# Six weight pairs loaded in the merge, products in TensorE's waits, and half of the branch weights issued earlier

## The chip, the core and the metric

The kernel runs on one core of a Trainium2 chip. The metric is device time in microseconds (us) of one execution; the time before is the median of three runs. One further execution was profiled, and all rows here are from it. The engines are TensorE (PE; PEld is its weight load), VectorE (DVE), ScalarE (ACT), GpSimd (POOL) and SyncE (SP, which issues most DMAs; "SPq" in rows). Each issues on its own, in program order, and they wait for each other by semaphores.

## What is computed

One decoder layer for 256 prompt tokens and 8 sample tokens (264 in all), model width 1024, in f32:

```
p = rms_norm(x) @ w_in
x = x + (sig(g_a) * (rwkv(p) @ w_br_a) + sig(g_b) * (nsa(p) @ w_br_b)) @ w_out
h = rms_norm(x)
logits = h @ w_router + b_router            # 32 experts, top 4, softmax
x = x + sum over the 4 experts:  top_w * (clamped_swiglu(h @ w_up[e] + b_up[e]) @ w_down[e] + b_down[e])
y = rms_norm(x)
```

`rwkv` is an RWKV-7 recurrence, `nsa` a sparse attention with a compressed, a selected and a window branch over cached keys. One expert has w_up of 1024x2048 (8.4 MB) and w_down of 1024x1024 (4.2 MB); all 32 are read, 403 MB. The sample group's window cache, shifted by a row, is an output too (a copy of 4.2 MB from memory to memory).

## The kernel before

The program is a row of stages; each is a block that begins and ends with a barrier of all engines. The order inside a block is written out by hand, engine by engine.

- `rwkv()` (projection and recurrence), then `attend()` with `compress` (compressed keys and values; `layer1`, the products L1135, and at its end L1188 and L1193), `attend_prompt` (begins with L1347, then gate products L1356 between attention products), `attend_samples` and `merge`.
- In `attend_samples` SyncE loads window rows, waits for `turned` to reach 16 and issues w_br_a and w_br_b (four loads each, L1479) into the half 0:P of every row of `sel`, where turned keys stood. TensorE turns the keys of eight (group, sample quad) units, and after them runs `branch_a(0)` (L1632) with w_br_a.
- In `merge` SyncE issues w_out (eight loads of [128, 8, 128], L1698) into the other half of `sel`, then x again and seven small loads (L1702, L1708, the last is c_dest), then the four quarters of w_up of expert 0 (L185). GpSimd waits for all of those but w_up and then issues the copy of the window cache (L1718). TensorE multiplies by w_br (L1764), by w_out (L1776), adds x (L1778), and makes partial logits (L1784) and sums of squares (L1789).
- In `experts` SyncE first issues the biases and a table `pick`, each twice (L1858 to L1860, semaphore `bias_in`, 96 in all), then w_down of experts 0 and 1 (four loads, L1854, in `sp_routes`), then w_up of expert 1, and then in a loop the weights of all others, each load when the slot is free. TensorE turns h (L2022), ranks the assignments (L2028, L2030), gathers expert 0's rows by a product (L2036), makes the table of slots (L2043), then runs expert 0: bias products (L2417), w_up products (L2430), later w_down (L2451) and the addition back (L2405). VectorE waits for `bias_in` after its one-hot work, copies `pick` twice (L1931, L1932), counts, and multiplies the gathered rows by the norm's gain (L1958); only then can L2430 begin.

Expert weights go through a ring of eight buffers `pairs` (16 KB per partition each, "ring" in rows): 0 to 3 hold the four quarters of one w_up, 4 to 7 two experts' w_down in halves. Pairs 4 to 7 lie over `sel`, so while w_out is there they can't be loaded. A quarter of w_up or a half of w_down is one DMA of 2 MB (2,097,152 bytes).

Of the kernel before, what the change touches and what calls it, by code (L numbers as in the profile page):

```python
# [29 lines left out]
P = 128  # L30
D = 1024
# [73 lines left out]
def build(nc, a, o, scratch):  # L105
    ctx = ExitStack()
    with ctx:
# [75 lines left out]
        def upper_weights(sp, e):  # L183
            for q in range(4):
                sp.dma_start(pairs[q][:], a["w_up"][0][e, 256 * q:256 * q + 256, :].rearrange("(p c) n -> p c n", c=2)).then_inc(ring_in[2 * q], 16)  # L185

# [31 lines left out]
        halves_of = (slice(0, HD), slice(HD, P))  # L218

# [403 lines left out]
        def rwkv_chunks(ar, q, bk, wc, av, br, vt, ktt, r, v):  # L623

            with nc.Block() as block, ExitStack() as st:
# [145 lines left out]
                def _(pe):  # L771
# [125 lines left out]
                    mm.then_inc(so, 1)  # L897

# [26 lines left out]
        def compress(sel, rows, qg, yb, B0, B1, gtok, bin_):  # L925


            with nc.Block() as block, ExitStack() as st:
# [196 lines left out]
                def _(pe):  # L1125
# [40 lines left out]
                    for b in range(NR // 2):  # L1166
                        if b % 2 == 0:
                            pe.wait_ge(C["raw_in"][b // 2], 32)
                        for r in (2 * b, 2 * b + 1):
                            if r >= 3:  # L1170
                                pe.wait_ge((fl_a, fl_d)[(r - 3) % 2], 2 * ((r - 3) // 2) + 1)
                            for kv in range(2):
                                for t in range(2):
                                    c0 = 256 * (r % 4) + P * kv
                                    mm = nc.tensor.transpose(banks[r % 3][:, TP * kv + P * t:TP * kv + P * t + P], raw[b // 2][:, t, c0:c0 + P], ident)
                            mm.then_inc(turned, 1)
                        if 2 * b in at_half:
                            setup(at_half.index(2 * b))
                        if b:
                            layer1(2 * b - 2)  # L1180
                            layer1(2 * b - 1)
                        if 2 * b + 1 in at_half:
                            setup(at_half.index(2 * b + 1))
                    layer1(NR - 2)
                    layer1(NR - 1)
                    pe.wait_ge(gl_ok, 2)
# [7 lines left out]
                    mm.then_inc(vc, 1)  # L1194

# [234 lines left out]
        def attend_samples(sel, qg, yb, B1, sc_, sel_in, br_in):  # L1430


            with nc.Block() as block, ExitStack() as st:
# [38 lines left out]
                def _(sp):  # L1472
# [3 lines left out]
                    sp.wait_ge(turned, 16)  # L1476
                    for i, n in enumerate("ab"):
                        for c in range(4):
                            sp.dma_start(sel[:, 4 * i + c, :, :, 0:P], a[f"w_br_{n}"][0][P * c:P * c + P, :].rearrange("p (a b n) -> p a b n", a=2, b=4)).then_inc(br_in[i], 16)  # L1479
# [198 lines left out]
        def merge(sel, br_in):  # L1678

            with nc.Block() as block, ExitStack() as st:  # L1680
# [11 lines left out]
                root_w = at("table_of_root", [P, 1], TEMPS)  # L1692
                wo_in, x_again = sem("mg_w_out_in"), sem("x_in_again")

                @block.sync
                def _(sp):
                    for c in range(KD):
                        sp.dma_start(sel[:, c, :, :, P:256], a["w_out"][0][P * c:P * c + P, :].rearrange("p (a b n) -> p a b n", a=2, b=4)).then_inc(wo_in, 16)  # L1698
# [11 lines left out]
                    upper_weights(sp, 0)  # L1710
# [43 lines left out]
                def _(pe):  # L1754
# [15 lines left out]
                    for m in range(KD):  # L1770
                        if m >= 2:
                            pe.wait_ge(oe, m - 1)
                        for c in range(KD):
                            if m == 0 and c == KD - 1:
                                pe.wait_ge(mix_ok, KD)
                            mmul(banks[m % 2][:, 0:T], sel[:, c, m // 4, m % 4, P:256], mix[:, c, :], start=(c == 0), stop=False)  # L1776
# [13 lines left out]
                    mm.then_inc(partd, 1)  # L1790

# [24 lines left out]
        def route(st):  # L1816
# [33 lines left out]
            def sp_routes(sp):  # L1850
                def down(e):
                    for j in range(2):
                        slot = 8 + 4 * e + 2 * j
                        sp.dma_start(pairs[slot // 2][:], a["w_down"][0][e, 512 * j:512 * j + 512, :].rearrange("(p b c) n -> p b (c n)", b=2, c=2)).then_inc(ring_in[slot], 16)  # L1854

# [5 lines left out]
                down(0)  # L1861
                down(1)
# [147 lines left out]
            def pe_routes(pe):  # L2010
                mmul = nc.tensor.matmul
                for lo, signal in ((1, msd), (0, lgd)):
# [3 lines left out]
                    mm.then_inc(signal, 1)  # L2016
                for i in range(6):
# [13 lines left out]
                mm.then_inc(rkd, 1)  # L2031
                for t, (_, n) in enumerate(TILES):
# [543 lines left out]
```

## Time and profile before

| what | us |
|---|---|
| median of three runs | 1440.2 |
| lowest and highest | 1438.92, 1441.64 |
| the profiled execution's own time | 1438.51 |
| its span in the trace | 1436.6 |

Mean granted TensorE clock 0.974 of full speed (full is 2.4 GHz, the lower level 0.5 of it is 1.2 GHz). TensorE is busy 93% of the span; of the chain that ended last, waits for DMAs are 33% and TensorE 32%. Stages in the profile: recurrence to 200 us, compressed branch to 273.7, prompt attention to 376, samples to 413.9, merge to 474.8, routing and experts from there. A row of a timeline gives the start, the length, the engine, the line and the operation, with the number of merged instructions; an f32 product counts as two. In brackets is the idle time before it and what ended it.

### The profile page before, as it was taken

How to read it: one execution, taken by the hardware profiler on the slowest of the kernel's cores; microseconds unless marked ns; L12 is line 12 of the kernel's file. 1: busy time of each engine (PE TensorE's matmuls, PEld its weight loads, DVE VectorE, ACT ScalarE, POOL GpSimd, SP SyncE). 2: the span in 40 equal slices, each digit the busy share in tenths (PEclk: the TensorE clock that was granted, in tenths of full speed). 3: DMA queues.
4: the chain of work that ended last, by engine and by line, in shares of the span. 5: the costliest groups of instructions: out<-in, count | busy, mean ns of one | idle time of the engine just before them, and what ended most of it. 6: DMA issues, size and time to landing. Idle time of an engine off the chain costs nothing.

```text
span 1436.6 us, 20588 instructions
## 1 busy us (share of the span) xinstructions
PE 1336.5 (93%) x8365; PEld 663.5 (46%) x8366; DVE 495.3 (34%) x1055; ACT 189.9 (13%) x407; POOL 101.9 (7%) x150
## 2 busy tenths in 40 slices
PE   6998879899999989999999999999999999999995
PEld 6887867687778523332333233333333333233231
DVE  3455556424551413232323223224222322233224
ACT  3221113323410300000000000000000000000001
POOL 1002032330000000000000000000000000000000
PEclk9999989899999999999999999999999999999998
DMA  6333248184488899999999999999999999999993
GB/s 213 118 93 91 64 108 269 41 276 146 150 215 341 337 431 429 431 430 431 431 431 431 431 431 432 430 430 431 431 429 433 430 432 431 431 432 430 431 431 133
DMA packets 94195, 479.94 MB, mean 334 GB/s; under 512 B 12740, under 2 KB 61110, under 8 KB 69176
## 3 DMA queue, kind: packets, MB, share of 16 engines
q1 hardware_dynamic: 85832, 452.00, 77.7%
q0 software_dynamic: 7600, 25.45, 4.9%
q10 hardware_dynamic: 704, 1.63, 0.3%
q8 instruction: 46, 0.75, 0.2%
q14 instruction: 13, 0.11, 0.0%
HBM read 478.60 MB, written 8.56 MB: 339 GB/s over the span
## 4 chain that ended last, share of the span: by engine, by line
DMA 33%; PE 32%; DVE 1%; issue 1%; ACT 0%; SPq 0%; DVEq 0%; ACTq 0%
DMA ring<-in_w_up 33%; PE bank L2430 18%; PE bank L2451 7%; PE bank L2405 2%; PE bank L2444 1%; PE bank L2417 1%; DVE x L2268 1%; PE bank L2387 1%; PE bank L2036 0%; PE bank L2022 0%; PE bank L2393 0%; DVE ring L2356 0%; PE bank L2043 0%; DVE x L2365 0%; PE bank L2014 0%
## 5 line engine op out<-in xcount | busy, mean ns | idle before, releaser
L2430 PE MATMUL bank<-ring,ex_work 128*64 128x512 f32 x2048 | 464.9, 603 | 24.4 <-DMA ring<-in_w_up 24.4
L2430 PEld LDWEIGHTS bank<-ring,ex_work 128*64 128x64 f32 x2048 | 140.9, 138 | 333.9 <-issue 274.3
L2451 PE MATMUL bank<-ring,ex_work 128*64 128x512 f32 x1024 | 233.6, 610 | 0.0
L2279 DVE TENSOR_SCALAR ex_work<-bank 128x512 f32<-128x512 f32 x32 | 22.1, 691 | 401.6 <-PE bank L2430 401.6
L2268 DVE TENSOR_TENSOR x<-bank,x 128x512 f32<-128x512 f32 (+1 forms) x192 | 117.2, 670 | 101.5 <-PE bank L2405 101.5
L2451 PEld LDWEIGHTS bank<-ring,ex_work 128*64 128x64 f32 x1024 | 72.2, 140 | 159.1 <-issue 159.1
L2405 PE MATMUL bank<-ex_work,ex_back 64*128 64x512 f32 x384 | 91.1, 606 | 1.5 <-ACT ex_work L2199 1.5
L558 PE MATMUL bank<-hT,w_group 128*128 128x264 f32 (+1 forms) x400 | 90.1, 387 | 0.0
L558 PEld LDWEIGHTS bank<-hT,w_group 128*128 128x128 f32 (+1 forms) x400 | 74.3, 186 | 14.7 <-issue 0.7
L2161 POOL DMA_INDIRECT ex_work<-scratch_h,ex_si x31 | 31.7, 1022 | 603.1 <-PE bank L2387 602.3
L2193 ACT ACTIVATE ex_work<-ex_work 128x512 f32<-128x512 f32 x32 | 20.1, 629 | 382.0 <-DVE ex_work L2279 382.0
L1356 PE MATMUL bank<-hT,w_cmp 128*128 128x264 f32 x256 | 67.8, 410 | 0.0
L2275 DVE COPY ex_pick_down<-ex_pick 64x64 f32 (+1 forms) x31 | 5.8, 187 | 162.4 <-PE bank L2451 162.4
L2405 PEld LDWEIGHTS bank<-ex_work,ex_back 64*128 64x128 f32 x384 | 34.4, 186 | 57.8 <-issue 49.8
L2199 ACT ACTIVATE ex_work<-bank 128x512 f32<-128x512 f32 x32 | 19.1, 597 | 262.8 <-PE bank L2451 262.8
L1356 PEld LDWEIGHTS bank<-hT,w_cmp 128*128 128x128 f32 x256 | 48.8, 201 | 7.4
L2189 ACT ACTIVATE ex_work<-bank 128x512 f32<-128x512 f32 x32 | 19.1, 597 | 227.4 <-PE bank L2393 227.4
L2444 PE MATMUL bank<-ex_bias,ex_pick_down 32*64 32x512 f32 x128 | 34.4, 612 | 15.9 <-DVE x L2268 14.5
L2417 PE MATMUL bank<-ex_bias,ex_pick_up 32*64 32x512 f32 x256 | 34.8, 612 | 0.6 <-DVE ex_pick_up L2271 0.6
L1776 PE MATMUL bank<-mixed,sel_rows 128*128 128x264 f32 x128 | 30.4, 391 | 0.0
L2387 PEld LDWEIGHTS bank<-masks,ex_work 128*128 128x128 f32 x124 | 17.3, 208 | 26.3 <-issue 23.5
L1958 DVE TENSOR_TENSOR ex_work<-bank,gain_columns 128x256 f32<-128x256 f32 x64 | 23.9, 413 | 9.5 <-PE bank L2387 8.0
(485 smaller groups left out, 1180.8 us busy)
## 6 DMA issues: line engine op xcount, KB each, us to landing
ring<-in_w_up SPq DMA_DIRECT2D x128, 2048.0 KB, 24.1
ring<-in_w_down SPq DMA_DIRECT2D x64, 2048.0 KB, 26.8
w_group<-in_w_in SPq DMA_DIRECT2D x12, 1024.0 KB, 5.3
w_cmp<-in_w_in SPq DMA_DIRECT2D x8, 1024.0 KB, 8.7
sel_rows<-in_w_out SPq DMA_DIRECT2D x8, 512.0 KB, 7.3
out_win_s<-in_state_win_kv POOLq DMA_DIRECT2D x1, 4088.0 KB, 28.9
x<-in_x_prompt SPq DMA_DIRECT2D x4, 512.0 KB, 4.9
win_rows<-in_state_win_kv SPq DMA_DIRECT2D x4, 512.0 KB, 4.9
```

Source lines behind the costliest of these rows:

```text
L558: mm = mmul(banks[2 + i % 4][0:n, 0:T], w[:, g % 3, kc, c:c + n], hT[:, kc, :], start=(kc == 0), stop=(kc == KD - 1))
L1356: mm = mmul(gate_bank(t)[:, 0:T], w[:, t // 2 % 2, kc, P * (t % 2):P * (t % 2) + P], C["hT"][:, kc, :], start=(kc == 0), stop=(kc == KD - 1))
L1776: mmul(banks[m % 2][:, 0:T], sel[:, c, m // 4, m % 4, P:256], mix[:, c, :], start=(c == 0), stop=False)
L1958: ins = nc.vector.tensor_tensor(B["xT"][:, :, gs], bank.rearrange("p (k s) -> p k s", k=4)[:, :, gs], R["gcol"][:, 2 * g:2 * g + 2].rearra ...
L2161: pool.indirect_dma_start(B["xg"][:], None, halves(scratch["h"]), bass.IndirectOffsetOnAxis(ap=B["si"][:, 0:1], axis=0), bounds_check=last ...
L2268: nc.vector.tensor_tensor(dst, banks[bank][0:n, :], dst, ALU.add).then_inc(S["added"], 1)
L2387: mm = nc.tensor.transpose(banks[6][:, P * k:P * k + P], B["xg"][:, 256 * (k // 2):256 * (k // 2) + 256].rearrange("s (p c) -> s c p", c=2 ...
L2405: mm = mmul(banks[bank], B["back"][hs, P * t:P * t + P], B["y"][hs, :], start=True, stop=True)
L2417: mmul(banks[n // 2][lo:lo + SLOTS, :], B["pick_up"][es, :], B["bias"][es, 512 * n:512 * n + 512], start=True, stop=False)
L2430: mm = mmul(banks[n // 2][lo:lo + SLOTS, :], B["xT"][:, k % 4, SLOTS * (k // 4):SLOTS * (k // 4) + SLOTS], slot_of(k)[:, 512 * n:512 * n + ...
L2444: mmul(banks[4][SLOTS * n:SLOTS * n + SLOTS, :], B["pick_down"][0:NEXP, :], B["bias"][0:NEXP, 2 * FF + 512 * n:2 * FF + 512 * n + 512], st ...
L2451: mm = mmul(banks[4][SLOTS * n:SLOTS * n + SLOTS, :], B["hT"][:, k % 4, SLOTS * (k // 4):SLOTS * (k // 4) + SLOTS], slot_of(8 + 4 * half + ...
```

## The change

- `merge` loads w_out into ring pairs 2 and 3, whole rows of 4 KB, not into `sel`. So `sel` is free once the branch products are done, and SyncE then (`ab`, KD) issues w_down of experts 0 and 1 into pairs 4 to 7. Of w_up of expert 0 only quarters 0 and 1 are issued before that, and quarters 2 and 3 after the output products (`od`, KD). `sp_routes` keeps the biases alone.
- `filled(bank, n)`: n products `ident` by 256 columns of `masks` into a bank that is not in use, at seven places.
- w_br_a is issued when eight units' keys are turned, w_br_b at sixteen as before.

```diff
-        def upper_weights(sp, e):
-            for q in range(4):
+        def upper_weights(sp, e, parts):
+            for q in parts:
...
+        def lower_weights(sp, e):
+            for j in range(2):
+                slot = 8 + 4 * e + 2 * j
+                sp.dma_start(pairs[slot // 2][:], a["w_down"][0][e, 512 * j:512 * j + 512, :].rearrange("(p b c) n -> p b (c n)", b=2, c=2)).then_inc(ring_in[slot], 16)
...
+        def filled(bank, n):
+            for _ in range(n):
+                nc.tensor.matmul(bank[:, 0:2 * P], ident, masks[:, 0:2 * P], start=True, stop=True)
...
                     mm.then_inc(so, 1)
+                    filled(banks[6], 4)
...
+                        if b == 1:
+                            filled(banks[3], 2)
                         if 2 * b in at_half:
...
                     layer1(NR - 1)
+                    filled(banks[2], 4)
                     pe.wait_ge(gl_ok, 2)
...
                     mm.then_inc(vc, 1)
+                    filled(banks[2], 2)
...
-                    sp.wait_ge(turned, 16)
                     for i, n in enumerate("ab"):
+                        sp.wait_ge(turned, 8 + 8 * i)
                         for c in range(4):
...
+                def wo(c):
+                    return pairs[2 + c // 4][:, c % 4 // 2, D * (c % 2):D * (c % 2) + D]
...
-                        sp.dma_start(sel[:, c, :, :, P:256], a["w_out"][0][P * c:P * c + P, :].rearrange("p (a b n) -> p a b n", a=2, b=4)).then_inc(wo_in, 16)
+                        sp.dma_start(wo(c), a["w_out"][0][P * c:P * c + P, :]).then_inc(wo_in, 16)
...
                     sp.wait_ge(outs.sem, 16 * 9)
-                    upper_weights(sp, 0)
+                    upper_weights(sp, 0, (0, 1))
+                    sp.wait_ge(ab, KD)
+                    for e in range(2):
+                        lower_weights(sp, e)
+                    sp.wait_ge(od, KD)
+                    upper_weights(sp, 0, (2, 3))
...
-                            mmul(banks[m % 2][:, 0:T], sel[:, c, m // 4, m % 4, P:256], mix[:, c, :], start=(c == 0), stop=False)
+                            mmul(banks[m % 2][:, 0:T], wo(c)[:, P * m:P * m + P], mix[:, c, :], start=(c == 0), stop=False)
...
                     mm.then_inc(partd, 1)
+                    filled(banks[7], 1)
...
-                down(0)
-                down(1)
...
                     mm.then_inc(signal, 1)
+                filled(banks[6], 2)
                 for i in range(6):
...
                 mm.then_inc(rkd, 1)
+                filled(banks[6], 2)
```

SyncE, from the end of the merge's small loads to the first load of expert 1; ring0 to ring3 are the quarters of w_up, ring4 to ring7 the halves of w_down. Before:

```order
L1708 DMA masks<-in_c_dest 128x24
L185 DMA ring0_49<-in_w_up 128x4096
L185 DMA ring1_50<-in_w_up 128x4096
L185 DMA ring2_51<-in_w_up 128x4096
L185 DMA ring3_52<-in_w_up 128x4096
L1680 UNCONDITIONAL_BRANCH
...
L1860 DMA ex_pick_4810<-in_c_pick 32x33
L1854 DMA ring4_53<-in_w_down 128x4096
...
L1854 DMA ring7_56<-in_w_down 128x4096
L2110 DMA ring0_49<-in_w_up 128x4096
```

And now:

```order
L1725 DMA masks<-in_c_dest 128x24
L185 DMA ring0_49<-in_w_up 128x4096
L185 DMA ring1_50<-in_w_up 128x4096
L190 DMA ring4_53<-in_w_down 128x4096
...
L190 DMA ring7_56<-in_w_down 128x4096
L185 DMA ring2_51<-in_w_up 128x4096
L185 DMA ring3_52<-in_w_up 128x4096
L1694 UNCONDITIONAL_BRANCH
...
L1878 DMA ex_pick_4830<-in_c_pick 32x33
L2128 DMA ring0_49<-in_w_up 128x4096
```

The w_down loads moved ahead of the stage's end, and so ahead of the biases; quarters 2 and 3 of w_up moved behind them.

TensorE at the end of the compressed branch, where the lines L1201 and L1206 are L1188 and L1193 of before, now:

```order
L1145 MATMUL bank<-sel_rows,w_cmp_late 128x265 x8
L227 MATMUL bank<-masks 128x256 x4
L1201 MATMUL bank<-sel_rows,w_cmp 64x264 x2
L1206 MATMUL bank<-w_cmp,sel_rows 128x64 x4
L1206 MATMUL bank<-w_cmp,sel_rows 8x64 x2
L227 MATMUL bank<-masks 128x256 x2
L938 UNCONDITIONAL_BRANCH
```

The two L227 rows are new; the rest stands as before.

## Rows read from the trace of the kernel before

**Rows 1.** The page, chain that ended last by line; then its last long wait.

```profile
DMA ring<-in_w_up 33%; PE bank L2430 18%; PE bank L2451 7%; PE bank L2405 2%; PE bank L2444 1%; PE bank L2417 1%; DVE x L2268 1%; PE bank L2387 1%; PE bank L2036 0%; PE bank L2022 0%; PE bank L2393 0%; DVE ring L2356 0%; PE bank L2043 0%; DVE x L2365 0%; PE bank L2014 0%
...
1318.41 25.93 DMA ring<-in_w_up
```

**Rows 2.** The page, GB/s moved in slices of 36 us.

```profile
GB/s 213 118 93 91 64 108 269 41 276 146 150 215 341 337 431 429 431 430 431 431 431 431 431 431 432 430 430 431 431 429 433 430 432 431 431 432 430 431 431 133
```

**Rows 3.** The issue of expert 1's first w_up quarter, with its time to landing.

```profile
L2110 SPq DMA_DIRECT2D ring<-in_w_up x1: 328/328/328, 496.3 to 496.3; - x1
...
DMA to landing us min/median/max: 14.6/14.6/14.6
```

**Rows 4.** Timeline of VectorE and TensorE before expert 0.

```profile
487.02 0.18 DVE L1931 COPY ex_pick_up<-ex_pick 64x64 f32<-64x64 f32 x1
...
489.92 0.76 DVE L1958 TENSOR_TENSOR ex_work<-bank,gain_columns 128x256 f32<-128x256 f32 x2 [1.47 <-PE bank L2050]
...
492.63 13.95 PE L2430 MATMUL bank<-ring,ex_work 128*64 128x512 f32 x64
```

**Rows 5.** Expert 0's w_up: issues 1 and 2, then all four, with landings.

```profile
L185 SPq DMA_DIRECT2D ring<-in_w_up x2: 432/432/433, 435.6 to 436.1; - x2
...
DMA to landing us min/median/max: 7.8/19.8/31.9
...
L185 SPq DMA_DIRECT2D ring<-in_w_up x4: 432/484/1137, 435.6 to 437.7; - x4
...
DMA to landing us min/median/max: 7.8/34.1/42.6
```

**Rows 6.** The window copy: its issue on GpSimd, and size and landing from the page.

```profile
439.18 0.68 POOL L1718 DMA_DIRECT2D out_win_s<-in_state_win_kv  x1 [24.32 <-DMA masks<-in_c_dest]
...
out_win_s<-in_state_win_kv POOLq DMA_DIRECT2D x1, 4088.0 KB, 28.9
```

**Rows 7.** Stretches; the last three columns are granted clock, DMA share, GB/s.

```profile
382.00:384.00 2.00, 2.00 (x23) 1.50 (x21) 1.58 (x3) 1.72 (x5) 0.00 (x0) 1.00 1.03 424
418.00:420.00 2.00, 2.00 (x10) 1.62 (x9) 1.51 (x4) 0.00 (x0) 0.00 (x0) 1.00 1.11 286
470.00:472.00 2.00, 2.00 (x28) 1.70 (x30) 0.43 (x1) 0.39 (x1) 0.00 (x0) 1.00 0.48 205
```

**Rows 8.** Timeline of SyncE's issues.

```profile
413.89 11.77 SPq L1698 DMA_DIRECT2D sel_rows<-in_w_out  x8
...
474.84 0.33 SPq L1858 DMA_DIRECT2D ex_bias<-in_b_up  x1
```

**Rows 9.** The last of the bias loads, the second pick table, with its landing.

```profile
L1860 SPq DMA_DIRECT2D ex_pick<-in_c_pick x1: 421/421/421, 477.1 to 477.1; - x1
...
DMA to landing us min/median/max: 6.9/6.9/6.9
```

**Rows 10.** Expert 1's first w_up products; the clock there; as many products later.

```profile
511.04 8.78 PE L2430 MATMUL bank<-ring,ex_work 128*64 128x512 f32 x32 [0.20 <-DMA ring<-in_w_up]
...
511.00:514.00 3.00, 2.96 (x8) 1.12 (x10) 0.00 (x0) 0.00 (x0) 0.00 (x0) 0.50 1.01 431
...
549.82 7.02 PE bank L2430 x32
```

**Rows 11.** Timeline of TensorE, four branch products of 264 columns.

```profile
433.61 1.94 PE L1764 MATMUL bank<-yaT,sel_rows 128*128 128x264 f32 x8
```

**Rows 12.** TensorE from the end of the compressed branch; then two stretches.

```profile
269.08 0.67 PE L1188 MATMUL bank<-sel_rows,w_cmp 128*64 128x264 f32 x4 [2.14 <-ACT sel_rows L1040]
269.83 1.43 PE L1193 MATMUL bank<-w_cmp,sel_rows 128*128 128x64 f32 x12
273.76 3.59 PE L1347 MATMUL bank<-KcT,pT 64*128 64x8 f32 x32 [2.51 <-PEq L928]
...
272.00:275.00 3.00, 1.24 (x12) 1.27 (x13) 0.00 (x0) 0.00 (x0) 1.11 (x6) 0.50 0.05 10
...
278.00:282.00 4.00, 4.00 (x11) 3.07 (x10) 1.43 (x6) 0.00 (x0) 0.20 (x2) 0.50 0.00 0
```

**Rows 13.** The wait for w_br_a on TensorE, and ScalarE's second exponential.

```profile
399.59 2.05 PE L1632 MATMUL bank<-yaT,sel_rows 128*128 128x264 f32 x8 [2.17 <-DMA sel_rows<-in_w_br_a]
...
401.86 0.72 ACT L1499 ACTIVATE bias<-bias,s_max 128x513 f32<-128x513 f32 x1 [0.99 <-DVE s_max L1558]
```

More of the change, by code:

```diff
@@ L1850, in sp_routes @@
             def sp_routes(sp):
[L1851 to L1854, printed above, removed]
                 for i in range(2):
```

## The prediction

> **What bounds the kernel now.** I read the views from the end backwards. The chain of work that ended last is a third wait for w_up ("DMA ring<-in_w_up 33%"), and its last such wait lasts 25.93 us and ends at 1344.3 [rows 1]. The slices of the page show 430 or so GB/s from 503 us to the end without a gap [rows 2]. So from expert 0 on one thing counts: when the stream of expert weights starts to be dense, and how many bytes are then left. A microsecond gained or lost before that point shows at the end one for one; what TensorE does faster among the experts shows nowhere. The point to follow is the landing of the first quarter of expert 1's w_up: issued at 496.3, landed 14.6 us later, at 510.9 [rows 3]. It is issued when TensorE has used the first quarter of expert 0, whose products begin at 492.63 [rows 4]; here it then stood 14.6 us in the queue, behind w_down of experts 0 and 1.
>
> **The part that everything turns on: the queue of SyncE in the merge.** The change moves 8 MB of w_down from behind the biases (issued from 474.84 [rows 8]) to the end of the branch products (about 437: their last group but one is at 433.6 [rows 11]), and half of w_up of expert 0 (4 MB) from 436 to the end of the output products. All are ahead of the biases now.
>
> How full is the queue there? Before, the four quarters of w_up were issued from 435.6 to 437.7. The first landed after 7.8 us (443.4), the second after 31.9 (468.0), the fourth after 42.6 (480.3) [rows 5]. At the rate of the expert phase a quarter of 2.1 MB takes 2.1 MB / 430 GB/s = 4.9 us. The second took 24.6. In that time ran the copy of the window cache, issued at 439.18 and landed 28.9 later, at 468.1, the very time of the second quarter [rows 6]. That copy is eight rows, and around 470 us the queues are busy 0.48 at 205 GB/s [rows 7]: half of the 16 DMA engines are idle and the other half, those with the copy, are behind. A load lands when its slowest engine is done, so those eight set the time, and to them the copy costs 24.6 - 4.9 = 19.7 us.
>
> Now the same for the change. (a) w_out goes into rows of 4 KB instead of pieces of 512 B. The pieces ran at 286 GB/s, window rows of 4 KB at 424 [rows 7]: 4.19 MB in 14.7 or in 9.9 us, 4.8 less. The eight w_out issues took SyncE 11.77 us [rows 8], and the small loads stood behind them; with less backlog these come sooner too. I take 5 us (4.3 to 6.3): the first quarter of w_up lands at 438.4. (b) Second quarter with the window copy: 24.6, so 463.0. (c) Four quarters of w_down, 4 x 4.9 = 19.6: 482.6. (d) The two held-back quarters of w_up, 9.8: 492.4. They may go once the output products are done, before 474.84 where the next stage's first issue stood, which is no limit; products 4 to 7 of expert 0 need them near 500, so they are no limit either. (e) The rows of h (264 x 4 KB, 1.08 MB) pass beside at some time, 2.5 us: 494.9. (f) The biases: the last of them, the second pick table, landed 6.9 us after 477.06 [rows 9], at 484.0, 3.7 us behind the last w_up quarter of then. So all six land at **498.6** in place of 484.0 (range 492 to 501; below 490 only if they need not queue behind the weights).
>
> Who waits for them? VectorE's `dve.wait_ge(S["bias_in"], 96)`. Queued behind it are the two pick copies (487.02 before), the counts and the gains multiply of expert 0, which began at 489.92 after 1.47 us of slack [rows 4]. TensorE's bias products need the pick copy, its w_up products the gains. From the landing to the first product it is 0.1 + (489.92 - 1.47 - 487.02) + 0.76 + 0.1 = 2.4 us: 501.0, against 492.63 before, **8.4 us late**. Breakeven is a landing at 490.2. TensorE is then idle for nearly 9 us, and its clock pays: after the gap before expert 1 the granted clock was 0.50 from 511 to 514 and 32 products took 8.78 us where 32 take 7.02 later [rows 10]. I add that **1.7 us** (0 to 2.7). So the first quarter of expert 1 is issued at 496.3 + 8.4 + 1.7 = 506.4. Nothing is queued then, and it lands like the first w_up quarter, 7.8 us later: 514.2, where it was 510.9. **Loading more in the merge costs 3.3 us**: the 14.6 us in the queue are saved to 7.8, but the queue starts 10.1 us later. Seen as bytes: the eight loaded engines save 5 us of w_out, and stand idle some 8 us between the biases and the next quarter, which they never did before.
>
> Whether the biases really queue behind the weights is what the sum hangs on. The row that bears on it: the last of them landed at 484.0, 3.7 us behind the last w_up quarter, while half of the engines had a backlog [rows 5, 9]. In order they land at 498.6 and the part costs 3.3 us; out of order it gains 6.8 (the first rival). The Trainium skill speaks for the first, against this change: by "DMA: Bandwidth & Descriptors", section Queues, rings and completion order, each DMA engine takes the descriptors of one issuing engine's ring in ring order. The trace agrees as far as the 3.7 us go, which is not far.
>
> After that point no gap opens: expert 1's fourth quarter lands at 514.2 + 14.7 = 528.9, and the stream would bring the next at 533.8. TensorE frees its slot at 511.04 + 10.1 + 3.7 = 524.8 (3.7 is 496.3 less 492.63), and with the 7.8 of a load that waits for nothing it could land at 532.6. That margin of 1.2 us is thin, so a gap of 0 to 2 us goes into the range.
>
> **Filled waits.** `filled(bank, n)` adds n products of 256 columns, which no one reads. Four of 264 columns take 1.94 us [rows 11], so one is 0.47. At the end of the compressed branch four (1.9 us) lie in a wait of 2.14 before L1188 and two (0.9) in the 2.51 before the next stage's first product [rows 12]: hidden, up to 0.1 us. What they give back is the clock: it was 0.50 from 272 to 282, through L1347 (3.59 us) and the first gate products [rows 12]. In the stage after it TensorE is the bound. TensorE worked from 273.8 to 282, 8.4 us, at half speed, 4.2 us lost. I expect it warm at 273.8, cold for two fifths of the 8.4 us, since L1347 has 8 columns and little to do (an estimate): lost 1.7 instead of 4.2, **a gain of 2.5** (0 to 3.4). The other fillers I cost at nothing: at the end of the recurrence TensorE waits for the next stage anyway, at `b == 1` for rel_bias, and the product after the next waits for gathered pages. Those in the routing could keep L2022 and L2036 warm, up to 1.7 us, but what ends last there is now the bias landing.
>
> **Half of the branch weights earlier.** TensorE waited 2.17 us for w_br_a before `branch_a(0)` (L1632) [rows 13]. That wait goes. Next late is VectorE's maximum: ScalarE's second exponential starts at 401.86 only and the products after it stand behind that [rows 13]. 0 (to 0.4). The loads stay behind the window rows in the same queue, so they disturb nothing.
>
> **Sum** against the profiled execution of 1438.5: -2.5 (clock) + 3.3 (biases) = +0.8, 1439.3. The median of the runs shown is 1.7 above the profiled one, so on its scale **1441.0**. The forecast's own range: 1437.5 to 1443.
>
> **Rivals.** *The biases are in time.* If they don't queue behind the weights (separate engines, or the window copy done earlier than I think), they land about 6 us after issue. Expert 0 starts at 492.6, the next quarter is issued at 496.3 and lands at 504.1 instead of 510.9: -6.8, with the clock's -2.5, 1438.5 - 9.3 = 1429.2, on the median's scale 1430.9. For it: the last pick table landed 6.9 us after its issue although a w_up quarter was still on its way [rows 5, 9]. Against: that quarter was nearly through by then, while now four to five are ahead. It decides when the landing is before 490.
> *The fillers don't hold the clock.* Then only the +3.3 stays: 1443.5; with the biases at 501 and 2.7 us of cold start it is +6.7, 1446.9. For it: the 1.43 us of L1193 didn't keep the clock before. It ends slower from a stream shift of 2.9 us up.
> *A gap behind expert 1* as above: +2 on the forecast, 1443.
>
> **Chances.** Forecast (and neighbours within it) 0.50; biases in time 0.17; fillers without effect 0.23; gap or later biases 0.10. A difference under 0.2% (2.9 us) can't be told from no change. Within: 0.50. Faster: the first rival and a tail where the landing is near 492 with the clock held, 0.20. Slower: 0.30. The range takes in the first rival's time and most of the third's: 1430.5 to 1447.
>
> **What would show it.** Right (each less the 2.5 us that the clock brings earlier): pick copies near 496, first w_up product of expert 0 near 498.5 with the clock at 0.5, DMA share near 0 between the two, expert 1's first quarter landing near 511.7. Gain right: granted clock 1.0 at 274 and L1347 near 2 us. Wrong if the pick copies stand at 487 or before, or if the first quarter of expert 1 lands before 508.

## The result, and the profile after

The change makes the kernel slower. Beside the kernel before on the same chip it took 1445.17 us (median of 7 runs, 1439.46 to 1450.25) against 1438.92 (7 runs), a ratio of 1.0044 with the interval 1.0025 to 1.0062. The profiled execution of the change is the shortest of its seven: 1439.46, with a span of 1437.4 us. A second set, below, gives 1.0027 (1.0011 to 1.0043).

Since the stages ahead of the merge end some microseconds earlier or later from one execution to the next, the traces are read in two parts here: up to the first load of w_out (413.89 before [rows 8], 407.39 after), and from there to the end of the span (1022.7 us before, 1030.0 after). The first part became shorter, the second longer by 7.3 us.

After the change, SyncE's issues of w_out and w_down; then w_down, the two held-back quarters of w_up and the two pick tables, each with the time from issue to landing (min/median/max):

```profile
407.39 3.83 SPq L1715 DMA_DIRECT2D ring<-in_w_out  x8
...
430.87 1.83 SPq L190 DMA_DIRECT2D ring<-in_w_down  x4
...
L190 SPq DMA_DIRECT2D ring<-in_w_down x4: 327/444/486, 430.9 to 432.3; - x4
DMA to landing us min/median/max: 31.5/38.2/44.7
...
L185 SPq DMA_DIRECT2D ring<-in_w_up x2: 328/380/433, 464.6 to 465.0; - x2
DMA to landing us min/median/max: 21.8/24.7/27.5
...
L1878 SPq DMA_DIRECT2D ex_pick<-in_c_pick x2: 413/440/468, 469.3 to 470.7; - x2
DMA to landing us min/median/max: 17.5/21.2/24.9
```

The second pick table is 4 KB and lands 24.9 us after its issue; before, it was 6.9 [rows 9]. It lands at 495.7, 3.2 us behind the last held-back quarter (465.0 + 27.5 = 492.5): it stood in the queue behind the weights. VectorE and TensorE show who waits (the bracket is idle time and its releaser):

```profile
495.71 0.19 DVE L1947 COPY ex_pick_up<-ex_pick 64x64 f32<-64x64 f32 x1 [14.22 <-DMA ex_pick<-in_c_pick]
...
495.95 1.98 PE L2435 MATMUL bank<-ex_bias,ex_pick_up 32*64 32x512 f32 x8 [9.45 <-DVE ex_pick_up L1947]
...
497.99 15.25 PE bank L2448 x64
```

and the page has a new member in the chain that ended last, 2% of the span, which [rows 1] doesn't have (L2448 is L2430 of before):

```profile
DMA ring<-in_w_up 28%; PE bank L2448 20%; PE bank L2469 8%; PE bank L2423 3%; DMA ex_pick<-in_c_pick 2%; PE bank L2462 1%; PE bank L2435 1%; PE bank L2405 1%; DVE x L2286 1%; PE bank L2411 0%; DVE ring L2374 0%; DVE x L2383 0%; DVE ex_work L1974 0%; DVE ex_work L2301 0%; DVE ex_work L2304 0%
```

Three stretches of the change (the last three columns are granted clock, DMA share, GB/s), to be held against 1.02 and 388 GB/s that the same engines moved over 477 to 503 us before:

```profile
476.00:484.00 8.00, 7.42 (x47) 4.61 (x43) 5.05 (x14) 6.01 (x10) 0.00 (x0) 0.97 1.01 229
...
484.00:495.00 11.00, 2.50 (x11) 2.19 (x10) 0.00 (x0) 0.00 (x0) 0.47 (x1) 0.50 0.49 196
...
496.00:500.00 4.00, 3.94 (x14) 1.02 (x16) 3.42 (x20) 0.00 (x0) 0.25 (x2) 0.50 0.00 0
```

First the DMA engines are all busy but move half of their rate (over 478 to 482 even less, 133 GB/s at share 0.98), then half of them have nothing to do, then all. The next load, expert 1's first quarter, is issued at 502.96 and lands 8.9 us later, at 511.9.

Where the change does gain: the end of the compressed branch on TensorE, with fillers (L227) in the waits. Against [rows 12], L1347 (now L1361) takes 1.95 us in place of 3.59, and the clock at 272 to 275 is 1.00:

```profile
266.07 1.99 PE L227 MATMUL bank<-masks 128*128 128x256 f32 x8
268.28 0.67 PE L1201 MATMUL bank<-sel_rows,w_cmp 128*64 128x264 f32 x4 [0.21 <-ACT sel_rows L1050]
...
270.37 1.13 PE L227 MATMUL bank<-masks 128*128 128x256 f32 x4
272.95 1.95 PE L1361 MATMUL bank<-KcT,pT 64*128 64x8 f32 x32 [1.45 <-PEq L938]
...
272.00:275.00 3.00, 2.05 (x33) 2.06 (x34) 0.00 (x0) 0.00 (x0) 1.61 (x8) 1.00 0.04 5
275.00:278.00 3.00, 3.00 (x8) 2.33 (x9) 1.92 (x8) 0.00 (x0) 2.15 (x10) 0.55 0.00 0
```

### The profile page after: what moved, and what is told of

The parts are those of the page before. It is cut to its first block, busy times and chain, and to the rows that moved or that the text cites. A ratio compares the mean times of both kernels' runs of the same rounds, so it can differ in the third digit from the quotient of the medians.

```text
span 1437.4 us, 20656 instructions
## 1 busy us (share of the span) xinstructions
PE 1335.6 (93%) x8399; PEld 662.7 (46%) x8400; DVE 494.7 (34%) x1055; ACT 189.8 (13%) x407; POOL 102.9 (7%) x150
## 4 chain that ended last, share of the span: by engine, by line
PE 35%; DMA 30%; DVE 2%; issue 1%; SPq 0%; ACT 0%; DVEq 0%; ACTq 0%
DMA ring<-in_w_up 28%; PE bank L2448 20%; PE bank L2469 8%; PE bank L2423 3%; DMA ex_pick<-in_c_pick 2%; PE bank L2462 1%; PE bank L2435 1%; PE bank L2405 1%; DVE x L2286 1%; PE bank L2411 0%; DVE ring L2374 0%; DVE x L2383 0%; DVE ex_work L1974 0%; DVE ex_work L2301 0%; DVE ex_work L2304 0%
## 5 line engine op out<-in xcount | busy, mean ns | idle before, releaser
L2448 PE MATMUL bank<-ring,ex_work 128*64 128x512 f32 x2048 | 465.2, 605 | 21.7 <-DMA ring<-in_w_up 21.5
L2448 PEld LDWEIGHTS bank<-ring,ex_work 128*64 128x64 f32 x2048 | 141.6, 138 | 331.4 <-issue 279.4
L1798 PE MATMUL bank<-mixed,ring 128*128 128x264 f32 x128 | 30.4, 391 | 0.0
## 6 DMA issues: line engine op xcount, KB each, us to landing
out_win_s<-in_state_win_kv POOLq DMA_DIRECT2D x1, 4088.0 KB, 28.9
```

The source lines that it names most:

```text
L1798: mmul(banks[m % 2][:, 0:T], wo(c)[:, P * m:P * m + P], mix[:, c, :], start=(c == 0), stop=False)
L2448: mm = mmul(banks[n // 2][lo:lo + SLOTS, :], B["xT"][:, k % 4, SLOTS * (k // 4):SLOTS * (k // 4) + SLOTS], slot_of(k)[:, 512 * n:512 * n + ...
```

## The experiments

All were timed in five rounds beside the kernel before, and ratios are to it. *The theory*: the biases and pick tables stand behind the weights in SyncE's queue, expert 0 waits for them, and the stream of weights then starts late. *Its rivals*: the early weights themselves do the harm (they slow the rest of the merge), or the fillers do.

### One order of the queue or another: e1 and e2

e1 is the change with the six loads of biases ahead of w_down (their tiles are made earlier, at the same place):

```
                     sp.wait_ge(ab, KD)
+                    sp.wait_ge(mix_ok, KD)
+                    for i in range(2):
+                        es = slice(NEXP * i, NEXP * i + NEXP)
+                        sp.dma_start(B["bias"][es, 0:2 * FF], a["b_up"][0]).then_inc(S["bias_in"], 16)
+                        ... (b_down and c_pick likewise; the same six leave sp_routes)
                     for e in range(2):
                         lower_weights(sp, e)
```

> The change, but the six loads of biases and pick tables are issued in the merge, ahead of w_down, once the mixing on VectorE is done (their place in memory is free from then). Theory (in order behind the weights, the biases land late and hold back expert 0): the pick copies stand near 481 where they stood at 495.7, there is no gap in the DMA share before expert 1, and the time is 8 to 10 us under the change, some 3 to 5 us under the kernel before. Rival (something else in the merge makes the change slow, such as the load of the engines that carry the window copy): pick copies early as well, but the time within 3 us of the change.

e2 leaves the biases in `sp_routes` and puts the two held-back quarters behind them:

```
                         lower_weights(sp, e)
-                    sp.wait_ge(od, KD)
-                    upper_weights(sp, 0, (2, 3))
 ...
+                upper_weights(sp, 0, (2, 3))    # in sp_routes, behind the biases
```

> The change, but the two held-back quarters of expert 0's w_up are issued behind the biases, at the start of the routing stage, instead of ahead of them. Same bytes, another order. Theory (order in the queue): the biases land 9 to 12 us earlier, near 485, expert 0 starts near 487 and waits at its fifth product for the quarters if at all; 5 to 8 us under the change. Rival (the biases are slow because all DMA engines are busy, whatever the order): they land within 3 us of 495.7, time unchanged.

Measured: e1 1432.11 us, 0.9949 (0.9934 to 0.9963); e2 1431.8 us, 0.9951 (0.9937 to 0.9966). The same bytes in another order: 0.8 to 0.95% (11 to 14 us) faster than the change by its two ratios, and 7 us faster than before. VectorE's pick copies, e2's and then TensorE's first w_up products, e2's and e1's:

```profile
488.92 0.19 DVE L1946 COPY ex_pick_up<-ex_pick 64x64 f32<-64x64 f32 x1 [4.20 <-DMA ex_pick<-in_c_pick]
...
491.20 15.68 PE L2447 MATMUL bank<-ring,ex_work 128*64 128x512 f32 x64
...
490.25 13.95 PE L2452 MATMUL bank<-ring,ex_work 128*64 128x512 f32 x64
```

In e1 nobody waits for the tables at all. So the cause is the order, and that is shown, not argued. Both gained more than I had expected (8 to 10 us under the change for e1, 5 to 8 for e2).

### The parts apart: e3 and e4

e3 is the change without any `filled(...)` (so it has the merge's loads and the earlier branch weights). e4 is the reverse: fillers and earlier branch weights, with the merge's loads, w_out and `down(0)`, `down(1)` as in the kernel before.

> The change without any of the fillers. Theory of the prediction: the clock is at half again from 272 to 282 and the stage before the samples starts 2.5 us later or more (up to 6, as the profile of the change had its stage starts 0.7, 0.8 and 6.4 us earlier than before); time 2.5 to 6 us over the change. Rival (the clock's falls are set by where they happen to fall, and the fillers do nothing): the same time as the change within 1.5 us.

> The kernel before plus the fillers and the earlier w_br_a: the change without the part on the merge's loads. Theory (the merge's loads cost, the fillers give): 2.5 to 6 us under the kernel before, so 9 to 12 under the change. Rival (fillers do nothing): the same as before within 1.5 us, and the merge's loads alone then cost 6.

Measured: e3 1447.36 us, 1.0057 (1.0042 to 1.0071), 8.2 us above before; e4 1436.79 us, 0.9989 (0.9977 to 1.0001), 1.6 below by the ratio. In e3 the copies wait longest:

```profile
504.06 0.19 DVE L1941 COPY ex_pick_up<-ex_pick 64x64 f32<-64x64 f32 x1 [15.93 <-DMA ex_pick<-in_c_pick]
```

The merge's loads cost some 8 us, the rest gives back about 2. The fillers are not the harm. For e4 I had expected 2.5 to 6 us, and its interval just takes in no gain at all.

### The change again

> The change itself, unaltered, beside the three others on one chip, since its seven times spread over 10.8 us. Both theories: about 1445 us, a ratio of 1.004 to the kernel before; in its trace TensorE's first product of expert 0 stands about 90 us behind the first load of w_out (90.6 in the trace of the change, 78.7 before).

1444.48 us (12 runs, 1438.44 to 1449.76), 1.0027 (1.0011 to 1.0043). From the first w_out load (409.79) to the first product (500.70) it is 90.9 us, and to the end of the span 1030.6: as in the first trace of the change.

### The window copy in sixteen rows: e5, e6, e9

```
-                    pool.dma_start(o["win_s"][0, :, 0:511]..., a["state_win_kv"][0, :, 1:512]...).then_inc(win_copied, 16)
+                    for lo, hi in ((0, 256), (256, 511)):
+                        pool.dma_start(o["win_s"][0, :, lo:hi]..., a["state_win_kv"][0, :, lo + 1:hi + 1]...).then_inc(win_copied, 16)
```

(and the wait for it is for 32.) e5b is the change with this, e6b is e1 with this, e9 the kernel before with this.

> The change with the window copy written as two DMAs, of 256 and 255 positions: sixteen rows where there were eight. Nothing else differs. Theory 1 (the copy lies on half of the DMA engines, and a load is done when its slowest engine is; this is what makes the biases late): the DMA share no longer stands near 0.5 between the copy's end and the biases; the second quarter of w_up and all behind it land some 10 us earlier (the copy's 19.7 us on eight engines become about 9.8 on sixteen), the pick copies stand near 81 us behind the first w_out load in place of 88.3, TensorE's wait goes, and the time falls from about 1445 to 1436-1439, ratio 0.998 to 1.001. Theory 2 (the biases are late by the mere number of bytes ahead of them): share stays as it was, pick copies near 88, time 1444-1446.

> e1 (the biases first) with the window copy in sixteen rows as well. Theory 1: at the issue of expert 1's first quarter the eight loaded engines still had a backlog in e1, so that quarter landed 10.8 us or more after its issue; with the copy spread it lands about 8 us after, and the time falls by up to 3 us against e1: 1429-1431, ratio 0.993. Theory 2 (that half of the engines is behind costs nothing once the biases are in time): 1432, ratio 0.995. Above 1434 would say that the spread copy disturbs the loads more than the narrow one.

> The kernel before, with nothing changed but the window copy in sixteen rows (two DMAs). The biases were never waited for there, so this asks what the copy on half of the engines cost by itself. Theory 1 (the stream of weights is set by its slowest engines): in the trace of before the queues are busy by half from 458 to 474 us, that is 16 us at half or 8 us of all engines; the first quarter of expert 1's w_up, which landed 14.6 us behind its issue, can land at best about 8 to 9 behind it, so 5 to 6.5 us of gain: about 1434, ratio 0.996. Theory 2 (half of the engines lost in this stretch cost nothing, since the loads have time until expert 1): 1440, ratio 1.000.

Measured: e5b 1433.06 us, 0.9962 (0.9948 to 0.9977); e6b 1431.72 us, 0.9939 (0.9925 to 0.9953); e9 1438.55 us, 0.9997 (0.9986 to 1.0008).

e5b: with one more DMA and nothing else the change goes from 0.3-0.4% above to 0.4% below before, 3 us further than the 1436 to 1439 us of its first theory. Its landing times, of the held-back quarters, then of the pick tables, and the wait:

```profile
L185 SPq DMA_DIRECT2D ring<-in_w_up x2: 328/380/433, 464.5 to 464.9; - x2
DMA to landing us min/median/max: 9.7/12.7/15.7
...
DMA to landing us min/median/max: 12.0/13.1/14.2
...
484.90 0.19 DVE L1948 COPY ex_pick_up<-ex_pick 64x64 f32<-64x64 f32 x1 [3.46 <-DMA ex_pick<-in_c_pick]
```

The copies stand 77.6 us behind the first w_out load, not 88.3: the copy on half of the engines cost the biases 10.7 us. The Trainium skill, "DMA: Bandwidth & Descriptors", section Why a DMA increments its semaphore by 16 and not by 1, has the rule: a DMA takes the largest number of engines, up to 16, that divides its slowest dimension on both sides; eight rows take eight. The trace of before agrees (share 0.48 [rows 7]). Each half of the split copy has eight rows again; that the two halves load all engines evenly is read from the share. The stretch of 460 to 470 us, in the change (where the held-back quarters are issued at 464.6) and then in e5b, whose merges began within 0.1 us of each other:

```profile
460.00:470.00 10.00, 8.67 (x73) 6.89 (x72) 1.96 (x9) 1.50 (x5) 0.00 (x0) 0.99 0.71 279
...
460.00:470.00 10.00, 8.67 (x73) 6.88 (x71) 2.02 (x9) 1.56 (x5) 0.00 (x0) 0.99 0.99 403
```

e9 was a miss, and a useful one: I had expected 5 us from the same edit in the kernel before, and it gave nothing. Its stretch of 474 to 482:

```profile
474.00:482.00 8.00, 6.18 (x53) 5.15 (x46) 4.25 (x24) 4.21 (x8) 0.00 (x0) 0.81 0.52 116
```

The queues run dry there: SyncE issues w_down only at 479.62, in the next stage, and the dense stream begins with that issue, whatever the copy did (expert 1's first quarter lands 14.0 us after its issue, before 14.6). So here engines that are behind cost only where somebody waits for their part. In the change that was the case (biases behind weights), before it was not.

e6b against e1 is inside the intervals and shows no gain, but its trace from the first w_out load to the end is 1017.4 us against 1019.3, and at 490 to 494 its queues are empty (share 0.08, 32 GB/s): what starts the stream now is TensorE, not a DMA.

### Is it the early w_down or the early biases? e8

e8b is e4 with the biases issued in the merge, behind the four quarters of w_up, and w_down where it was before.

> Fillers and the earlier branch weights as in the change, but w_out, w_up and w_down as before (all of expert 0's w_up in the merge, w_down of both experts behind the routing's start); the biases alone go earlier, behind w_up in the merge. It asks whether loading six pairs in the merge is worth anything once the biases are in time. Theory 1 (the bytes that the loaded engines have moved by the first product count): the stream is dense from about 475 on in either order, so it ends as e1 does or up to 2 us later: 1432-1434, ratio 0.995-0.997. Theory 2 (the early w_down is the gain of e1 and e2, the order of the biases only its condition): no better than fillers and branch alone, 1436-1437, ratio 0.998-0.999.

1436.59 us, 0.9983 (0.9971 to 0.9995), as e4. So the early biases alone bring nothing, since nobody waited for them before; what brings the 4.9 us between the ratios of e8b and e1 (2.3 between their traces, in the table's last column) is w_down (and w_out's longer rows) in the merge, and the biases' place is the condition for it. Of my two theories the second one held.

### Fillers, branch weights and a colder clock once more: e10, e11, e12

Three edits of e6b, in one set: without fillers (e10), with `sp.wait_ge(turned, 16)` ahead of both halves of the branch weights as before (e11), and with four more fillers in the routing (e12):

```
                 mm.then_inc(first_d, 1)
+                filled(banks[6], 4)
```

> e6b (biases first, copy in sixteen rows) without the filled waits. If they are worth the 2.5 us that the prediction gave them: 1434-1435, ratio 0.996. If their worth came only from the wait for the biases (a colder TensorE in the routing): no more than e6b, 1431.7, 0.994.

> e6b with the first half of the branch weights issued where it was before, when all 16 units' keys are turned. The prediction gave the earlier issue nothing, 0.4 us at most: then 1432, ratio 0.994, as e6b. If the 2.17 us wait before the branch products comes back and lies on the path: 1434, ratio 0.9955.

> e6b with four more filled products of 256 columns in the routing, behind the products of the first 64 rows, where TensorE waits for the dispatch table. In e6b's trace TensorE's granted clock fell to 0.50 from about 491 to 494 and the first 64 w_up products of expert 0 took 15.65 us where 13.95 stand at full clock, while the DMA engines had nothing to do from 491 to 496. If the clock is what starts the stream late: 64 products in about 14 us, the first quarter of expert 1 issued some 1.7 us earlier, 1430, ratio 0.993. If the fillers stand in the way of the products behind them, or the clock falls all the same: 1432 or more.

Measured: e10 1433.49 us, 0.9961 (0.9948 to 0.9974); e11 1430.44 us, 0.9937 (0.992 to 0.9955); e12 1431.16 us, 0.9937 (0.9922 to 0.9952). The fillers are worth 0.0022 to 0.0024, 3.2 to 3.5 us, though e10's interval overlaps a little with those of e6b, e11 and e12. The earlier branch weights are worth nothing. The four added fillers did not hold the clock; e12's first 64 products and the stretch in which they begin:

```profile
491.11 15.65 PE L2454 MATMUL bank<-ring,ex_work 128*64 128x512 f32 x64
...
490.00:494.00 4.00, 4.00 (x18) 1.09 (x19) 3.36 (x14) 0.00 (x0) 1.31 (x2) 0.70 0.00 0
```

Nor was there a wait for them to fill: in e6b, as in e12, TensorE is busy without a break from 482 to 494. In e12's trace the added products take 1.99 us, and the first w_up product comes 80.0 us behind the first w_out load, where it is 77.5 in e6b; their medians don't differ.

The fillers of the change in the routing are another matter. From the first pick copy to the first w_up product it is 5.6 to 5.7 us in the traces without them (before, e9, e10) and 4.1 in those with them where nobody waits for the tables (e1, e4, e8b, e6b, e11): the six products that gather expert 0's rows take 4.59 us in e10 and 2.98 in e6b.

e6b, e11 and e12 are one kernel as far as these measurements tell, 0.6% faster than the kernel before and about 1% faster than the change.

### All traces in one table

Worked out from the timelines, one execution each: "gates" is from the load of cmp_seen (end of the compressed branch) to that of the window rows. "Half clock" is how long in the first 40 us of that stage TensorE was granted 0.50 instead of 1.00, worked out from the mean granted clock of its first and its second 20 us (to some 0.4 us); after them it is 1.00 in all. The others count from the first w_out load, to the first w_up product of expert 0, to the issue of expert 1's first quarter, and to the end of the span.

| kernel | gates | half clock | first product | issue | end of span |
|---|---|---|---|---|---|
| before | 102.3 | 8.4 + 6.8 | 78.7 | 82.4 | 1022.7 |
| e9, before, copy in 16 rows | 102.5 | 8.8 + 6.8 | 78.8 | 82.5 | 1022.8 |
| e4, fillers and branch only | 98.3 | 3.6 + 3.6 | 78.1 | 81.8 | 1020.8 |
| e8b, e4 with early biases | 98.4 | 3.6 + 3.6 | 77.5 | 81.2 | 1021.6 |
| the change | 96.7 | 3.6 + 0 | 90.6 | 95.6 | 1030.0 |
| a1, the change again | 98.4 | 3.6 + 3.6 | 90.9 | 96.7 | 1030.6 |
| e3, the change, no fillers | 99.9 | 6.8 + 3.6 | 91.5 | 96.5 | 1030.6 |
| e5b, the change, copy in 16 rows | 96.7 | 3.6 + 0 | 81.0 | 87.3 | 1021.7 |
| e2, held-back quarters behind | 98.4 | 3.6 + 3.6 | 80.6 | 86.0 | 1020.3 |
| e1, biases first | 98.3 | 3.6 + 3.6 | 78.3 | 82.0 | 1019.3 |
| e6b, both | 100.0 | 6.8 + 3.6 | 77.5 | 82.9 | 1017.4 |
| e10, e6b, no fillers | 100.3 | 7.6 + 3.6 | 80.3 | 84.0 | 1018.2 |
| e11, e6b, late branch weights | 98.4 | 3.6 + 3.6 | 77.5 | 82.9 | 1018.1 |
| e12, e6b, more fillers | 96.7 | 0 + 3.6 | 80.0 | 85.4 | 1019.6 |

Two columns are worth a look. The last goes by the place of the weights and biases: about 1030 with the biases behind, 1021 to 1023 with w_down late (and 1021.7 in e5b), 1017 to 1020 with w_down early and the biases in time or nearly so (e2, with a wait of 4.20 us, has 1020.3). And the "gates" column, which the queue in the merge can't touch, is 102.3 to 102.5 in the two kernels with neither fillers nor early branch weights, 99.9 to 100.3 with early branch weights but no fillers, and 96.7 to 98.4 in all with fillers but one (e6b, 100.0). The branch weights are not what moved it: they are loaded behind this stage, and e11 has 98.4 without their earlier issue. What moved it is TensorE's clock. Take half of the "half clock" time from "gates", and 94.7 to 94.9 us are left in all fourteen. With the fillers the clock is at 1.00 up to the stage's start in every trace, and falls there in e6b, some 2 us later in most, and not in the first 20 us in e12; without them it has fallen some 2 to 4 us before the stage begins. A second fall, between 24 and 34 us into the stage, takes 6.8 us in before and e9, 0 in two traces and 3.6 in the ten others. e3 and e10 run the same program as before up to the window rows, so the 2 us by which they stand under it are no edit's doing; what sets the length of the two falls is open.

## Why the prediction was right, and where not

The time of the change, 1445.17, lies in the range given (1430.5 to 1447), and the mechanism was the right one: the biases queue behind the weights, expert 0 waits for them, and the stream starts late. But the likeliest case, "within 0.2%", did not come true, and the slower case had only 0.3.

**(a) w_out in 4 KB rows, 5 us: right for the issue, not for the landing.** SyncE's issues of w_out fell from 11.77 us to 3.83, and the first w_up quarter was issued 16.7 us behind the first w_out load, where it was 21.7 before (435.6 - 413.89): 5.0 less. But it took 14.1 us to land in place of 7.8 [rows 5], so it landed at 30.8 (424.1 + 14.1 - 407.39) where I had put 24.5, even later than the 29.5 of before. From 418 to 430 us the queues were full at 344 GB/s: what SyncE had issued ahead of it was not yet through.

**(b), (c) second quarter, window copy, w_down: 5.4 us too long.** I had w_down done at 482.6, 68.7 us behind the first w_out load; it landed at 432.3 + 44.7 = 477.0, 69.6 behind. That (a) to (c) fit together is two errors that cancel: the first landing was 6.3 us late, and from it to the last of w_down it took 38.8 us, not 24.6 + 19.6 = 44.2. Which part of (b) and (c) was shorter, the landings don't tell.

**(d), (e) held-back quarters and rows of h: the step that failed.** 9.8 + 2.5 = 12.3 us were set; from 477.0 to 492.5 it is 15.5, of which the first quarter took 9.4. The stretch of 476 to 484 shows why: all 16 engines busy at 229 GB/s, where the stream runs at 430; in 8 us that loses 3.7. I had put the rows of h there at full rate. In e1 the first two parts of the rows of h are written from 479.29 and 482.06, and the engines that are busy there run near full rate (416 GB/s at share 0.99, then 311 at 0.78 over 482 to 484); what is slow is where the biases are (issued 437.0 to 439.2, the last landed 29.0 later, at 468.2). e1's two stretches:

```profile
462.00:464.00 2.00, 2.00 (x11) 1.71 (x10) 0.00 (x0) 0.00 (x0) 0.00 (x0) 1.00 1.01 208
...
474.00:482.00 8.00, 8.00 (x55) 7.14 (x54) 5.70 (x24) 6.25 (x12) 0.00 (x0) 0.79 0.99 416
```

So the term that was too small is most likely that of the biases (2 x 384 KB), whose bytes my sum had only in the 3.7 us of (f): the eight engines without a backlog seem to reach them while the others still carry weights, and meanwhile all are busy and move little. That is read from where the slow stretches lie (in the kernel before too: its biases are issued from 474.84, and over 478 to 480 it moves 203 GB/s at share 1.05); no run has the biases left out.

**(f) Biases +3.7 behind the last quarter: right** (495.7 - 492.5 = 3.2). **2.4 from landing to first product: right** (497.99 - 495.7 = 2.3). **Cold clock: right.** The clock is 0.50 at 496 to 500, 64 products take 15.22 us where 13.95 stood, and the issue comes 4.97 us behind the first product (502.96 - 497.99); I had 3.7 + 1.7 = 5.4. **Landing of the next quarter, 7.8:** 8.9.

**The sum of the merge.** From the first w_out load to the landing of expert 1's first quarter: 97.0 before [rows 3, 8], 100.3 predicted, 104.5 measured (511.9 - 407.39). The term of +3.3 should have been +7.5, that is 4.2 more: 0.9 by the end of (c), 3.2 from (d) and (e), 1.1 from the last landing, less 1.0 from (f) and what lies between. The rest of the run follows it: the spans from there on differ by 7.3 (1030.0 against 1022.7), and e3, which has this term alone but for the branch weights, is 8.2 slower. That no gap opens behind expert 1 was right.

**Fillers, -2.5: right in size.** e10 gives 3.2 to 3.5, e4 1.6, e3 against the two ratios of the change 1.9 to 4.3 (0.0013 and 0.0030 of 1440); none of these differences is clear of its intervals, but all point the same way. At the place that the term was about, the change's trace has 3.6 us at half clock in place of 8.4, so 1.8 lost in place of 4.2, as I had it. The stage gained 5.6 there all the same, because the second fall of the clock, which the prediction doesn't have, was missing in this execution; a1 has it again, and gains 3.9. The fillers in the routing, which I put at nothing because the biases would end last, give 1.6 us to the first product once the biases are in time. The rival "the fillers don't hold the clock" falls in the place that I had named (1.00 at 272 to 275; it then fell at 275.3 to 278.7 all the same), and holds in another: TensorE's idle time in the routing, where it waits for the biases. **Branch weights, 0: right** (e11).

**The chances.** With +7.5 - 2.5 the sum is +5.0, and 1445.2 on the median's scale; 1445.17 was measured, beside a kernel before that was 1.3 us lower than the median I had started from. Against that one the change costs 6.3 us where I forecast 0.8, so the range was met at its upper end. The signs came closer than the working deserves, by luck: pick copies at 495.7 (I said 496), first product at 497.99 (498.5), expert 1's first quarter at 511.9 (511.7). The first w_out load stood 6.5 us earlier than before, where I had 2.5, and the merge took 4.2 us more. "Biases in time" is refuted. The rival that named the right time was the one with the higher landing, to which I gave 0.10 as "gap or later biases", because I priced later biases only through the range of single terms (492 to 501). On the scale of the trace of before, the landing was 413.89 + 88.3 = 502.2, just outside of it.

**What I did not see.** That the same loads in another order make the kernel 0.5% faster. I wrote "breakeven is a landing at 490.2" and had the number on the table: it is the price of being late, and it falls away as soon as six small issues are written ahead of four large ones.

## What to carry to other kernels

Where a queue is filled earlier with bulk loads, go through the small loads behind it that somebody will soon wait for, and issue these first: here the order of six small loads decided between +0.3 to 0.4% and -0.5%. Before pricing a half-idle stretch of the DMA engines, ask whether anyone waits for the half that is behind: the same copy on eight engines delayed the biases by 10.7 us in the change, and cost the kernel before nothing. Before placing fillers, check that the wait is still there: in e12 it was not, and they only came in between. Then look at what starts the dense stream (here an issue, a table, or TensorE in turn), since only that start and the bytes left behind it count.

## What the runs showed of the hardware that I had not expected

- The DMA engines can all be busy and yet move half: 208 GB/s (e1) and 229 (the change) at share 1.01 in stretches where the biases are under way (2 x 384 KB). What makes them slow was not tried.
- In a stage of about 100 us where TensorE is the bound, fourteen traces differ by up to 5.8 us, and half of the time at the granted clock 0.50 accounts for all but 0.3 us of that. Part of that differs between executions of one kernel (96.7 and 98.4 in the change's two traces).
- One more DMA for the same bytes (16 rows for 8) shortens the copy from 28.9 us to 18.8 and 21.2 for its halves, and the biases land 10.7 us earlier.
- Four fillers more in the routing did not keep TensorE at full clock in e12 (0.70 over 490 to 494), while in e1, without them, it stayed at 1.00 from 482 on; what decides it there stays open.
- Single executions of the change spread by 10.8 and 11.3 us, those of e1 and e2 by 3.1 and 2.8 (with 7, 12, 5 and 5 executions). The clock's second fall is one source, 1.7 us between the two traces of the change; the rest can't be read from one or two traces of each.
